# A fused two-block transformer kernel: one depthwise chunk moved to DVE, the others three chunks behind the projection, and unread products in TensorE's waits

## The chip, the cores and the metric

The kernel runs on one NeuronCore of one Trainium2 chip. The metric is the device time of one execution in microseconds; lower is better.

## The reference

256 tokens of width 1024, all in float32, pass through two blocks of two layers each. The part that the change touches is in the second block:

```python
def _conformer_conv(h, w_pw1, b_pw1, w_dw, b_dw, ln_g, ln_b, w_pw2, b_pw2):
    u = h @ w_pw1 + b_pw1                                   # 1024 -> 2048
    u = u[..., :D_MODEL] * jax.nn.sigmoid(u[..., D_MODEL:])
    c = depthwise_conv(u, w_dw, taps=31, centred) + b_dw    # each channel by itself
    c = jax.nn.silu(_layernorm(c, ln_g, ln_b))
    return c @ w_pw2 + b_pw2

def second_block(x):
    for i in range(2):
        x = x + 0.5 * rmsnorm(swiglu(rmsnorm(x)))           # half feed-forward
        m = conformer_conv(rmsnorm(x)) if i == 0 else diff_attention(rmsnorm(x))
        x = x + rmsnorm(m)
        x = x + 0.5 * rmsnorm(swiglu(rmsnorm(x)))
```

The first block has a layer with a compressed and windowed attention, one with a latent attention, and a feed-forward behind each. The differential attention is the third attention of the kernel.

## The kernel before

**Numbers.** Products have to be near float32. Every weight w is split into a high part that TensorE reads in one pass (`whi`) and the rest (`wlo`), every operand into `hthi` and `htlo`, and each product is made of three. ScalarE makes the high parts, DVE the low parts.

**Weights.** All weights come as a stream of 176 units of 128 x 3072 through `raw`, `whi` and `wlo`, two slots each, in two pieces: a (2048 columns) and b (1024). SyncE loads a piece when DVE has made the low part of the one before in its slot. Each engine's program is an order written out by hand; semaphores tie them together. `hi_a`, `hi_b` (ScalarE) and `lo_a`, `lo_b` (DVE) are the two splits of a unit.

**Borders.** Between two stages x has to be complete, is transposed by TensorE in four groups of four (`x_operand`, `operand_ahead`, L899), gained and split by ScalarE (L508) and DVE (L1436), and is then the operand. Groups 0 and 1 come first; group 2 stands in front of the first products, group 3 in front of the products of k = 2. At the borders numbered 5 to 9 (`AFTER_POST`: op_conv, op_f4, op_f5, op_qkv, op_f6) x is the sum of the old x and a normed output, which DVE adds in a first and a second half (L1510); groups 0 and 1 wait for the first, group 2 for the second. op_f4 and op_f6 follow a mixer, the others a feed-forward.

**Convolution stage.** The projection has 16 output groups q of 128 channels; q = 2c and 2c+1 are value and gate of chunk c (8 chunks). They lie in units as `PW1 = [[0,1,2],[3,4,5],[6,7,8],[9,10,11],[12,13],[14,15]]`. When q = 2c+1 is done, DVE scales the bank (L1876), ScalarE takes the sigmoid (L815), DVE multiplies (L1879) into `conv_u`. The depthwise convolution of a chunk is 32 small products on TensorE (`convolve`, L1272): GpSimd stores the chunk to DRAM (`gated`, L405) and loads it four times, shifted by a column each, into one of three slots (`stacked`, L412), so that a product covers four taps of 32 channels. The tap weights are eight loads of 512 KB, made long before. `convolve(c)` stands in TensorE's order two chunks behind the projection (`BEHIND = 2`). ScalarE adds the bias (`biased`, L803); the layer norm's mean and variance are products with a matrix of 1/1024 (L1281, L1321). Then DVE and ScalarE make the operand of the second pointwise product (`htlo`, L1897).

**Unread products.** `busy(cnt)` issues products whose results nobody reads; it stands once in the second attention's preparation (L891).

**Third attention.** 16 items; per item two score products on TensorE (L1098), bias and maximum on DVE (L1581), exponentials on ScalarE (L597), mixing on DVE (L1610), two transposes (L1107) and two value products (L1139). Scores run two items ahead. ScalarE is the busiest there.

```python
            for w, chunks in enumerate(PW1):
                ...
                    if q % 2 and q // 2 >= BEHIND:
                        convolve(q // 2 - BEHIND)
            taken("r_conv", 1)
            mean_of(range(0, 8 - BEHIND - 1))
            for c in range(8 - BEHIND, 8):
                convolve(c)
            mean_of(range(8 - BEHIND - 1, 8)).then_inc(ev["mean_done"], 1)
```

Of the kernel before, what the change touches and what calls it, by code (L numbers as in the profile page):

```python
# [60 lines left out]
BEHIND = 2  # L61
# [17 lines left out]
        ("qnope", 1), ("b_pw1", 16), ("ln_g", 8), ("ln_b", 8), ("b_dw", 8),  # L79
# [110 lines left out]
def build(nc, stream, cols_d, rows_d, wide_d, taps_d, x_d, const_d, out_d):  # L190
    ctx = ExitStack()
    with ctx:
# [38 lines left out]
        extra = sb("extra", [P, STACK * UPITCH])  # L231
# [7 lines left out]
        def col(name, i=0):  # L239
# [14 lines left out]
        tap_w = [(tr[:, 2048 + 1024 * c:3072 + 1024 * c] if c < 6 else att[:, 1024 * (c - 6):1024 * (c - 5)])  # L254
                 .rearrange("p (g q n) -> p g q n", g=STACK, q=SHIFTS) for c in range(8)]
# [4 lines left out]
        conv_bank = [acc[c % 4][:, (c // 4) * T:(c // 4 + 1) * T] for c in range(8)]  # L260
# [75 lines left out]
            "qpe_ready", "mean_done", "centred", "sq_ready", "var_done",  # L336
# [46 lines left out]
        def _(pool):  # L383
# [8 lines left out]
            for n in range(7):  # L392
                if n == 0:
                    pool.wait_ge(ev["cm1"], 1)
                if n == 2:
                    pool.wait_ge(s_ol, 16)
                    pool.wait_ge(s_x, 12)
                    for c in range(8):

                        pool.wait_ge(s_useb, U_F2 + 2 + 2 * c)  # L400
                        pool.dma_start(tap_w[c].rearrange("p g q n -> p (g q n)"), taps_d[c]).then_inc(s_tap, 16)
                if n == 3:
                    for c in range(8):
                        pool.wait_ge(s_glu, c + 1)
                        pool.dma_start(gated[c], conv_u[:, c, :]).then_inc(s_gtd, 16)  # L405
                        if c == 0:
                            pool.wait_ge(s_std, RSTD["n5"] + 1)
                        if c >= SLOTS:
                            pool.wait_ge(s_dw, c - SLOTS + 1)
                        pool.wait_ge(s_gtd, 16 * (c + 1))  # L410
                        for j in range(STACK):
                            pool.dma_start(stacked[c % SLOTS][j * GROUP:(j + 1) * GROUP, :, 0:UPITCH - STACK],  # L412
                                           gated[c].rearrange("(g p) n -> p g n", g=STACK)[:, :, j:j + UPITCH - STACK])\
                                .then_inc(s_stk[c % SLOTS], 16)
# [10 lines left out]
        def _(act):  # L425
# [374 lines left out]
            def biased(c):  # L800

                act.wait_ge(s_dw, c + 1)
                nc.scalar.activation(conv_c[:, c, :], conv_bank[c], ACT.Identity, bias=col("b_dw", c)).then_inc(s_cc, 1)  # L803

            for w, chunks in enumerate(PW1):
# [5 lines left out]
                for q in chunks:  # L811
                    if q % 2:
# [4 lines left out]
                        if c > BEHIND:  # L817
# [59 lines left out]
        def _(pe):  # L877
# [31 lines left out]
            def operand_ahead(name, src, there):  # L909
# [12 lines left out]

                one(0)
                one(1)
                return ready

            def x_operand(name, m):
# [6 lines left out]
                return operand_ahead(name, lambda t, c: x[:, t, c * P:(c + 1) * P], there)  # L934
# [138 lines left out]
            def attention(kind):  # L1073
# [70 lines left out]
                scores(1)  # L1144
                for i in range(cnt + 2):
# [118 lines left out]
            def convolve(c):  # L1264

                pe.wait_ge(s_tap, 16 * 8)
                pe.wait_ge(s_stk[c % SLOTS], 16 * STACK * (c // SLOTS + 1))
                if c >= 4:
                    pe.wait_ge(s_cc, c - 3)
                for q in range(SHIFTS):  # L1270
                    for g in range(STACK):
                        ins = nc.tensor.matmul(conv_bank[c][g * GROUP:(g + 1) * GROUP, :], tap_w[c][:, g, q, :],  # L1272
                                               stacked[c % SLOTS][:, g, STACK * q:STACK * q + T],
# [3 lines left out]
            def mean_of(chunks_):  # L1277

                for c in chunks_:
                    pe.wait_ge(s_cc, c + 1)  # L1280
                    ins = nc.tensor.matmul(mean_bank, ones, conv_c[:, c, :], start=c == 0, stop=c == 7)  # L1281
# [3 lines left out]
            for w, chunks in enumerate(PW1):  # L1285
# [3 lines left out]
                for m, q in enumerate(chunks):  # L1289
# [32 lines left out]
            ins.then_inc(ev["var_done"], 1)  # L1322

# [18 lines left out]
            attention("diff")  # L1342
# [8 lines left out]
        def _(dve):  # L1351
# [513 lines left out]
            V.memset(conv_u[:, :, PAD + T:], 0.0)  # L1865
# [220 lines left out]
```

## Time and profile before

| | |
|---|---|
| time, median of 3 runs | 1826.09 us (1823.67 to 1826.11) |
| the profiled execution | 1820.93 us, of it span 1819.1 us |
| TensorE busy | 1700.5 us, 93% of the span |
| DVE, ScalarE busy | 1135.2 us (62%), 821.7 us (45%) |
| GpSimd busy | 37.8 us (2%) |
| mean granted TensorE clock | 0.970 of full speed |

The span runs from the first to the last instruction of the profiled execution. A granted clock of 1.00 is TensorE at 2.4 GHz, 0.50 is 1.2 GHz; a value between is the mean over a stretch in which it changed. The convolution stage lies between 931 and 1067 us, the third attention between 1544 and 1578 us. In a row of a timeline, "x8" are eight instructions in one row, the second number is what they took together, and the bracket says how long the engine was idle before it and for whom.

### The profile page before, as it was taken

How to read it: one execution, taken by the hardware profiler on the slowest of the kernel's cores; microseconds unless marked ns; L12 is line 12 of the kernel's file. 1: busy time of each engine (PE TensorE's matmuls, PEld its weight loads, DVE VectorE, ACT ScalarE, POOL GpSimd, SP SyncE). 2: the span in 40 equal slices, each digit the busy share in tenths (PEclk: the TensorE clock that was granted, in tenths of full speed). 3: DMA queues.
4: the chain of work that ended last, by engine and by line, in shares of the span. 5: the costliest groups of instructions: out<-in, count | busy, mean ns of one | idle time of the engine just before them, and what ended most of it. 6: DMA issues, size and time to landing. Idle time of an engine off the chain costs nothing.

```text
span 1819.1 us, 29989 instructions
## 1 busy us (share of the span) xinstructions
PE 1700.5 (93%) x11719; PEld 1564.4 (86%) x11719; DVE 1135.2 (62%) x1646; ACT 821.7 (45%) x1236; POOL 37.8 (2%) x65
## 2 busy tenths in 40 slices
PE   7969999998999999999988789998999989789998
PEld 7947799997878999999987589997999989689997
DVE  4777566655756666766563366666656655666665
ACT  4466454335645433543352454334434354754333
POOL 0000000000000000000003110000000000000000
PEclk9979999999999999999999989999999999889999
DMA  7610255453425655454536345454445445045454
GB/s 272 207 60 1 70 178 201 175 182 128 141 71 199 227 208 204 154 208 173 187 140 195 106 162 208 173 191 166 174 175 201 177 137 185 3 139 208 173 194 152
DMA packets 56366, 295.88 MB, mean 163 GB/s; under 512 B 6640, under 2 KB 7024, under 8 KB 33776
## 3 DMA queue, kind: packets, MB, share of 16 engines
q1 hardware_dynamic: 52224, 281.33, 43.1%
q0 software_dynamic: 4080, 13.70, 2.5%
q8 instruction: 42, 0.69, 0.2%
q14 instruction: 20, 0.16, 0.0%
HBM read 292.77 MB, written 2.23 MB: 162 GB/s over the span
## 4 chain that ended last, share of the span: by engine, by line
PE 87%; DVE 6%; ACT 5%; issue 1%; DMA 1%; POOL 0%; DVEq 0%; SPq 0%; ACTq 0%; POOLq 0%
PE bank L880 18%; PE bank L882 18%; PE bank L881 18%; PE bank L1069 9%; PE bank L1038 3%; PE bank L1040 3%; PE bank L1042 3%; PE bank L899 2%; PE bank L1272 2%; PE bank L1127 1%; PE bank L1085 1%; PE bank L1107 1%; ACT att L597 1%; ACT whi L440 1%; DVE x L1510 1%
## 5 line engine op out<-in xcount | busy, mean ns | idle before, releaser
L880 PE MATMUL bank<-hthi,whi 128*128 128x256 f32 x2144 | 608.2, 284 | 0.0
L882 PE MATMUL bank<-hthi,wlo 128*128 128x256 f32 x2144 | 607.3, 283 | 0.0
L881 PE MATMUL bank<-htlo,whi 128*128 128x256 f32 x2144 | 607.3, 283 | 0.0
L1365 DVE TENSOR_TENSOR wlo<-raw,whi 128x2048 fp32r<-128x2048 f32 x175 | 401.1, 2292 | 103.1 <-ACT whi L440 103.1
L880 PEld LDWEIGHTS bank<-hthi,whi 128*128 128x128 f32 x2144 | 411.8, 192 | 6.7 <-issue 2.1
L881 PEld LDWEIGHTS bank<-htlo,whi 128*128 128x128 f32 x2144 | 411.8, 192 | 4.7
L882 PEld LDWEIGHTS bank<-hthi,wlo 128*128 128x128 f32 x2144 | 411.8, 192 | 0.0
L440 ACT ACTIVATE whi<-raw 128x2048 fp32r<-128x2048 f32 x175 | 334.0, 1908 | 38.7 <-PE bank L882 27.3
L523 ACT ACTIVATE tr<-tr 128x256 f32<-128x256 f32 x132 | 55.2, 418 | 641.8 <-DVE tr L1454 641.8
L1454 DVE TENSOR_TENSOR tr<-bank,rb 128x512 f32<-128x512 f32 x132 | 91.2, 691 | 225.6 <-PE bank L882 225.4
L1371 DVE TENSOR_TENSOR wlo<-raw,whi 128x1024 fp32r<-128x1024 f32 x174 | 212.2, 1219 | 28.4 <-ACT whi L448 28.2
L880 PE MATMUL bank<-whi,hthi 128*128 128x384 f32 (+4 forms) x520 | 175.1, 337 | 14.7 <-DVE htlo L1897 6.9
L448 ACT ACTIVATE whi<-raw 128x1024 fp32r<-128x1024 f32 x174 | 181.5, 1043 | 0.4 <-PE bank L882 0.3
L881 PE MATMUL bank<-wlo,hthi 128*128 128x384 f32 (+4 forms) x520 | 171.9, 331 | 0.0
L882 PE MATMUL bank<-whi,htlo 128*128 128x384 f32 (+4 forms) x520 | 171.8, 330 | 0.0
L880 PEld LDWEIGHTS bank<-whi,hthi 128*128 128x128 f32 (+1 forms) x520 | 99.5, 191 | 17.6 <-issue 10.1
L1038 PE MATMUL bank<-whi,hidhi 128*128 128x512 f32 x288 | 113.4, 394 | 0.0
L1040 PE MATMUL bank<-wlo,hidhi 128*128 128x512 f32 x288 | 112.9, 392 | 0.0
L1042 PE MATMUL bank<-whi,hidlo 128*128 128x512 f32 x288 | 112.1, 389 | 0.0
L881 PEld LDWEIGHTS bank<-wlo,hthi 128*128 128x128 f32 (+1 forms) x520 | 99.6, 191 | 0.0
L882 PEld LDWEIGHTS bank<-whi,htlo 128*128 128x128 f32 (+1 forms) x520 | 99.1, 191 | 0.0
L1457 DVE TENSOR_TENSOR tr<-tr 128x256 f32<-128x256 f32 x132 | 56.2, 426 | 63.9 <-ACT tr L523 63.9
(250 smaller groups left out, 1999.7 us busy)
## 6 DMA issues: line engine op xcount, KB each, us to landing
raw<-in_stream SPq DMA_DIRECT2D x176, 1024.0 KB, 5.5
raw<-in_stream SPq DMA_DIRECT2D x176, 512.0 KB, 3.6
wide<-in_wide POOLq DMA_DIRECT2D x7, 512.0 KB, 4.3
tr<-in_taps POOLq DMA_DIRECT2D x6, 512.0 KB, 3.6
xn<-gated POOLq DMA_DIRECT2D x12, 142.0 KB, 4.0
proj<-gated POOLq DMA_DIRECT2D x12, 142.0 KB, 3.1
gated<-proj POOLq DMA_DIRECT2D x8, 144.0 KB, 3.1
extra<-gated POOLq DMA_DIRECT2D x8, 142.0 KB, 3.4
```

Of the source, the lines that this page charges most:

```text
L440: nc.scalar.activation(whi[:, s, 0:UA], raw[:, s, 0:UA], ACT.Copy).then_inc(s_hia, 1)
L448: nc.scalar.activation(whi[:, s, UA:UNIT], raw[:, s, UA:UNIT], ACT.Copy).then_inc(s_hib, 1)
L880: nc.tensor.matmul(out, whi_, mhi, start=start, stop=False)
L881: nc.tensor.matmul(out, whi_, mlo, start=False, stop=False)
L882: return nc.tensor.matmul(out, wlo_, mhi, start=False, stop=stop)
L1038: nc.tensor.matmul(acc[2 * t + j][:, :], hidhi[:, b, lhs], whi[:, s, sl], start=start, stop=False, skip_group_check=True)
L1040: nc.tensor.matmul(acc[2 * t + j][:, :], hidhi[:, b, lhs], wlo[:, s, sl], start=False, stop=False, skip_group_check=True)
L1042: ins = nc.tensor.matmul(acc[2 * t + j][:, :], hidlo[:, b, lhs], whi[:, s, sl], start=False, stop=stop, skip_group_check=True)
L1069: ins = nc.tensor.matmul(acc[2 * t + j][:, :], a[:, 1, lhs], w[:, s, sl], start=False, stop=False, skip_group_check=True)
L1365: V.tensor_tensor(wlo[:, s, 0:UA], raw[:, s, 0:UA], whi[:, s, 0:UA].bitcast(F32), ALU.subtract)\
L1371: V.tensor_tensor(wlo[:, s, UA:UNIT], raw[:, s, UA:UNIT], whi[:, s, UA:UNIT].bitcast(F32), ALU.subtract)\
L1454: V.tensor_tensor(gu[:, j, :].rearrange("p (h n) -> p h n", h=2), gate_up_bank[j], both, ALU.mult)\
```

## The change

Five things are altered.

1. `BY_DVE = 1`: chunk 0 of the depthwise convolution is computed by DVE, 31 instructions on 128 x 256 (`conv_taps`), each adding one shifted and weighted copy to `conv_c`. They stand in DVE's order in runs of five (`AHEAD`) behind the gate product of chunks 1 to 6, and the last one behind chunk 7's. Chunk 0 is no longer stored, loaded and multiplied by TensorE.
2. `BEHIND = 3`: the other seven chunks' products stand three chunks behind the projection; the mean products are spread between them; the one of chunk 0 waits for the new event `conv_early`.
3. The third slot of `stacked` lies in `att` in place of `extra`, and the tap weights of chunk 7 in the other part of `att`.
4. `busy` takes the operand that it reads and the bank that it writes. Unread products are added: at the five borders of `AFTER_POST`, 18 in front of group 0 and 10 behind group 1; 40 behind the variance products; 24 in the third attention behind the scores of items 0 and 1; 24 behind the third attention.
5. The constants `cols` have 31 more columns, the tap weights of chunk 0.

```diff
-BEHIND = 2
+BY_DVE = 1
+AHEAD = 5
+BEHIND = 3
...
-        extra = sb("extra", [P, STACK * UPITCH])
...
-            xn[:, :, :].rearrange("p t n -> p (t n)")[:, 0:STACK * UPITCH], proj[:, 4352:4352 + STACK * UPITCH], extra[:, :])]
+            xn[:, :, :].rearrange("p t n -> p (t n)")[:, 0:STACK * UPITCH], proj[:, 4352:4352 + STACK * UPITCH], att[:, 1024:1024 + STACK * UPITCH])]
...
-                    for c in range(8):
+                    for c in range(BY_DVE, 8):
+                        n_ = c - BY_DVE
                         pool.wait_ge(s_glu, c + 1)
                         pool.dma_start(gated[c], conv_u[:, c, :]).then_inc(s_gtd, 16)
-                        if c == 0:
+                        if n_ == 0:
                             pool.wait_ge(s_std, RSTD["n5"] + 1)
-                        if c >= SLOTS:
-                            pool.wait_ge(s_dw, c - SLOTS + 1)
-                        pool.wait_ge(s_gtd, 16 * (c + 1))
+                        if n_ >= SLOTS:
+                            pool.wait_ge(s_dw, n_ - SLOTS + 1)
+                        pool.wait_ge(s_gtd, 16 * (n_ + 1))
...
-                        if c > BEHIND:
+                        if c - BEHIND - 1 >= BY_DVE:
                             biased(c - BEHIND - 1)
...
-            def busy(cnt):
+            def busy(cnt, of=hthi, out=gub[1]):
 
                 for _ in range(cnt):
-                    nc.tensor.matmul(gub[1][:, 0:T], hthi[:, 0, 0:P], hthi[:, 1, :], start=True, stop=True)
+                    nc.tensor.matmul(out[:, 0:T], of[:, 0, 0:P], of[:, 1, :], start=True, stop=True)
...
+                busy(spare[0], hidhi)
                 one(0)
                 one(1)
+                busy(spare[1], hidhi)
                 return ready
...
-                return operand_ahead(name, lambda t, c: x[:, t, c * P:(c + 1) * P], there)
+                return operand_ahead(name, lambda t, c: x[:, t, c * P:(c + 1) * P], there,
+                                     (18, 10) if m in AFTER_POST else (0, 0))
...
                 scores(0)
                 scores(1)
+                busy(spare, hidhi)
                 for i in range(cnt + 2):
...
-                    if q % 2 and q // 2 >= BEHIND:
+                    if q % 2 and q // 2 - BEHIND >= BY_DVE:
                         convolve(q // 2 - BEHIND)
             taken("r_conv", 1)
-            mean_of(range(0, 8 - BEHIND - 1))
-            for c in range(8 - BEHIND, 8):
-                convolve(c)
-            mean_of(range(8 - BEHIND - 1, 8)).then_inc(ev["mean_done"], 1)
+            convolve(5)
+            mean_of(range(BY_DVE, 4))
+            convolve(6)
+            pe.wait_ge(ev["conv_early"], 1)
+            mean_of(range(0, BY_DVE))
+            mean_of(range(4, 6))
+            convolve(7)
+            mean_of(range(6, 8)).then_inc(ev["mean_done"], 1)
             for c in range(8):
                 if c % 2 == 0:
                     pe.wait_ge(ev["sq_ready"], c // 2 + 1)
                 ins = nc.tensor.matmul(var_bank, ones, conv_s[:, c, :], start=c == 0, stop=c == 7)
             ins.then_inc(ev["var_done"], 1)
+            busy(40, hidhi)
...
-            attention("diff")
+            attention("diff", 24)
+            busy(24, hidhi, acc[3])
             step(U_WO, ready=operand_ahead("op_wo", lambda t, c: diff_o[:, t, c * P:(c + 1) * P],
...
+            def conv_taps(k0, k1, ready=None):
+
+                for k in range(k0, k1):
+                    for c in range(BY_DVE):
+                        w = col("w_dw", k * BY_DVE + c)
+                        if k == 0:
+                            ins = V.tensor_scalar(conv_c[:, c, :], conv_u[:, c, 0:T], w, col("b_dw", c), ALU.mult, ALU.add)
+                        else:
+                            ins = V.scalar_tensor_tensor(out=conv_c[:, c, :], in0=conv_u[:, c, k:k + T], scalar=w,
+                                                         in1=conv_c[:, c, :], op0=ALU.mult, op1=ALU.add)
+                    if ready is None or k < k1 - 1:
+                        own(ins)
+                if ready is not None:
+                    ins.then_inc(ready, 1)
...
+                        if c == BY_DVE:
+                            dve.wait_ge(s_glu, BY_DVE)
+                        if BY_DVE <= c < 7:
+                            conv_taps((c - BY_DVE) * AHEAD, (c - BY_DVE + 1) * AHEAD)
+            conv_taps((7 - BY_DVE) * AHEAD, TAPS, ready=ev["conv_early"])
             dve.wait_ge(ev["mean_done"], 1)
```

## Rows read from the trace of the kernel before

**Rows 1.** The page, part 1: busy time and share of the span, by engine

```profile
PE 1700.5 (93%) x11719; PEld 1564.4 (86%) x11719; DVE 1135.2 (62%) x1646; ACT 821.7 (45%) x1236; POOL 37.8 (2%) x65
```

**Rows 2.** Waits of TensorE: in total us, times, longest us

```profile
PE bank L899 <- DVE x L1510: 28.7, 10, 4.5
...
PE bank L899 <- DVE proj L1935: 4.2, 1, 4.2
...
PE bank L1272 <- issue: 1.8, 1, 1.8
```

**Rows 3.** Windows: us; busy PE, PEld, DVE, ACT, POOL; granted clock; DMA share, GB/s

```profile
935.00:937.40 2.40, 0.00 (x0) 0.01 (x1) 2.28 (x5) 0.82 (x3) 0.00 (x0) 0.64 0.31 111
...
1034.50:1041.30 6.80, 0.00 (x1) 0.00 (x0) 3.75 (x5) 4.13 (x7) 0.00 (x0) 0.76 0.00 0
...
1543.26:1546.67 3.41, 3.41 (x21) 2.96 (x19) 1.96 (x8) 3.29 (x7) 0.00 (x0) 1.00 0.92 310
```

**Rows 4.** Timeline of TensorE at the border before op_f5: start, us, instruction

```profile
1268.99 1.56 PE L899 MATMUL bank<-const,x 128*128 128x128 f32 x8 [3.13 <-DVE x L1510]
...
1272.91 1.08 PE L899 MATMUL bank<-const,x 128*128 128x128 f32 x4 [2.36 <-DVE x L1510]
...
1277.04 0.36 PE L1009 MATMUL bank<-hthi,whi 128*128 128x256 f32 x1
```

**Rows 5.** Timeline of TensorE: four small products at the high clock

```profile
949.26 0.60 PE L942 MATMUL bank<-const,rs 128*128 128x128 f32 x4
949.62 0.36 PE L880 MATMUL bank<-hthi,whi 128*128 128x256 f32 x1
```

**Rows 6.** The chain that ended last: unread products in the second attention's preparation

```profile
488.19 3.58 PE bank L891 x30
```

**Rows 7.** Timeline of TensorE at op_qkv and at the output projection

```profile
1470.08 1.09 PE L899 MATMUL bank<-const,x 128*128 128x128 f32 x4 [2.63 <-DVE x L1510]
...
1475.26 0.42 PE L880 MATMUL bank<-whi,hthi 128*128 128x384 f32 x1
...
1585.18 1.09 PE L899 MATMUL bank<-const,proj 128*128 128x128 f32 x4 [1.14 <-DVE htlo L1436]
...
1590.62 0.61 PE L880 MATMUL bank<-whi,hthi 128*128 128x384 f32 x1
```

**Rows 8.** Timeline of TensorE at the start of the third attention

```profile
1544.10 3.69 PE L1098 MATMUL bank<-tr 128*128 128x256 f32 x16
...
1548.37 0.44 PE L1107 MATMUL bank<-const,att 128*128 128x128 f32 x2 [0.57 <-DVE att L1610]
```

**Rows 9.** Timeline of TensorE: the first three depthwise chunks

```profile
963.78 4.93 PE L1272 MATMUL bank<-xn,tr 128*32 128x256 f32 x64 [5.29 <-DMA xn<-gated]
...
974.58 3.66 PE L1272 MATMUL bank<-proj,tr 128*32 128x256 f32 x64
...
984.12 3.66 PE L1272 MATMUL bank<-extra,tr 128*32 128x256 f32 x64
```

**Rows 10.** Timeline of DVE between the first projection chunks

```profile
954.45 2.29 DVE L1365 TENSOR_TENSOR wlo<-raw,whi 128x2048 fp32r<-128x2048 f32 x1 [0.58 <-ACT whi L440]
...
959.80 0.48 DVE L1879 SCALAR_TENSOR_TENSOR proj<-tr,cols 128x256 f32<-128x256 f32 x1 [0.58 <-ACT tr L815]
...
960.75 1.23 DVE L1371 TENSOR_TENSOR wlo<-raw,whi 128x1024 fp32r<-128x1024 f32 x1 [0.46 <-ACT whi L448]
```

**Rows 11.** Timeline of GpSimd: the depthwise stage's DMA issues

```profile
955.13 2.22 POOL L412 DMA_DIRECT2D xn<-gated  x4 [2.11 <-DMA gated<-proj]
...
964.20 2.19 POOL L412 DMA_DIRECT2D proj<-gated  x4 [4.94 <-DMA gated<-proj]
...
974.33 2.19 POOL L412 DMA_DIRECT2D extra<-gated  x4 [7.38 <-DMA gated<-proj]
...
995.81 0.56 POOL L405 DMA_DIRECT2D gated<-proj  x1 [3.82 <-DVE proj L1879]
...
998.42 2.19 POOL L412 DMA_DIRECT2D extra<-gated  x4 [2.04 <-DMA gated<-proj]
```

More of the change, by code:

```diff
@@ L78 @@
         ("b1", 4), ("pos", 32), ("w2", 256), ("kv_c_norm", 2), ("q_a_norm", 3), ("knope", 1),
[L79 removed]
+        ("qnope", 1), ("b_pw1", 16), ("ln_g", 8), ("ln_b", 8), ("b_dw", 8), ("w_dw", TAPS * BY_DVE),
         ("subln", 1)]
@@ L252, in build @@
         conv_r = proj[:, 6400:6912].rearrange("p (c n) -> p c n", c=2)
[L254 to L255 removed]
+        tap_w = {c: (tr[:, 2048 + 1024 * (c - BY_DVE):3072 + 1024 * (c - BY_DVE)] if c < 7 else att[:, 0:1024])
+                 .rearrange("p (g q n) -> p g q n", g=STACK, q=SHIFTS) for c in range(BY_DVE, 8)}
         stacked = [v.rearrange("p (g n) -> p g n", g=STACK) for v in (
[L258 removed]
+            xn[:, :, :].rearrange("p t n -> p (t n)")[:, 0:STACK * UPITCH], proj[:, 4352:4352 + STACK * UPITCH], att[:, 1024:1024 + STACK * UPITCH])]
         gated = nc.dram_tensor("gated", (8, P, UPITCH), F32, kind="Internal").ap()
[L260 removed]
+        conv_bank = {c: acc[(c - BY_DVE) % 4][:, (c - BY_DVE) // 4 * T:((c - BY_DVE) // 4 + 1) * T] for c in range(BY_DVE, 8)}
         mean_bank, var_bank = tp[0][:, 0:T], tp[1][:, 0:T]
@@ L335, in build @@
             "ckv_ready", "qa_ready", "k2_sq", "k2_ss", "q2_sq", "q2_ss", "k2n_ready", "q2n_ready", "kpe_ready",
-            "qpe_ready", "mean_done", "centred", "sq_ready", "var_done",
+            "qpe_ready", "conv_early", "mean_done", "centred", "sq_ready", "var_done",
             "conv_std", "lny_ready", "conv_hi", "conv_lo",
@@ L800, in biased @@
             def biased(c):
-                act.wait_ge(s_dw, c + 1)
+                act.wait_ge(s_dw, c - BY_DVE + 1)
                 nc.scalar.activation(conv_c[:, c, :], conv_bank[c], ACT.Identity, bias=col("b_dw", c)).then_inc(s_cc, 1)
@@ L907, in operand, with operand_ahead @@
                        lambda q: [(P, P, src(t, 2 * q + j)) for j in range(min(2, nchunks - 2 * q)) for t in range(NT)])
-            def operand_ahead(name, src, there):
+            def operand_ahead(name, src, there, spare=(0, 0)):
                 def one(q):
@@ L1071, in down_prev, with attention @@
                 ins.then_inc(s_useb, 1)
-            def attention(kind):
+            def attention(kind, spare=0):
                 base, cnt = ITEM0[kind], NITEM[kind]
@@ L1264, in convolve @@
             def convolve(c):
[L1266 to L1269, printed above, removed]
+                n_ = c - BY_DVE
+                pe.wait_ge(s_tap, 16 * (8 - BY_DVE))
+                pe.wait_ge(s_stk[n_ % SLOTS], 16 * STACK * (n_ // SLOTS + 1))
+                if n_ >= 4:
+                    pe.wait_ge(s_cc, n_ - 3)
                 for q in range(SHIFTS):
@@ L1279, in mean_of @@
                 for c in chunks_:
-                    pe.wait_ge(s_cc, c + 1)
-                    ins = nc.tensor.matmul(mean_bank, ones, conv_c[:, c, :], start=c == 0, stop=c == 7)
+                    if c >= BY_DVE:
+                        pe.wait_ge(s_cc, c - BY_DVE + 1)
+                    ins = nc.tensor.matmul(mean_bank, ones, conv_c[:, c, :], start=c == BY_DVE, stop=c == 7)
                 return ins
```

11 lines of the change are left out of this document (6 added, 5 removed).

## The prediction, made before the change was timed

> **What bounds the kernel now.** I read the page first: TensorE is busy for 93% of the span, DVE for 62% [rows 1], so the kernel goes as fast as TensorE's queue, and only its idle time and its slow time can be won. The view of waits, TensorE alone, then shows where it is idle: 28.7 us in ten waits for x at the block borders, 4.2 us after the third attention, 1.8 us before the last depthwise products [rows 2], and, by TensorE's timeline, 5.29 us before the first ones [rows 9]. The reader is to see that each is a chain on DVE, ScalarE or the DMA queues that TensorE can't shorten by itself. The third view is the granted clock by stretch: in the second wait of a border its mean is 0.64, so it falls from 2.4 to 1.2 GHz there, and in the layer norm's wait of 6.8 us, with TensorE at 0.00, it falls too, to a mean of 0.76 [rows 3]. So a wait costs twice: while it lasts, and in the products behind it.
>
> **Borders (five times, before op_conv, op_f4, op_f5, op_qkv, op_f6).** The change adds 18 unread products in front of the wait for the first half of x and 10 behind the first eight transposes. One such product takes 3.58/30 = 0.12 us at 2.4 GHz [rows 6], so they take 2.2 us and 1.2 us. The waits that hide them are 3.13 and 2.36 us at the border of op_f5 [rows 4]; the longest are 4.5 us [rows 2]. Nothing queued behind them comes later, as long as the clock is high when they begin, and it is, since the block before ends in back-to-back products. Cold they would take about twice as long, 10 then still under 2.36.
> What they may win: from the third group of transposes to the products behind the fourth the trace has 1277.04 - 1272.91 = 4.13 us [rows 4]: two groups of four transposes and twelve 128x256 products. At 2.4 GHz a group of four costs 949.62 - 949.26 = 0.36 us [rows 5], so the same work is 0.36 + 12 x 0.12 + 0.36 = 2.16 us, 2.0 us less. The third group itself can't start earlier, as it waits for DVE's second half of x. ScalarE and DVE make the operand a group at a time behind the transposes, so they move with them, and in the feed-forward loop behind them the view of waits has none for another engine. For op_qkv with 384 columns: 1475.26 - 1470.08 = 5.18 us [rows 7]; twelve products at 0.33 cold and, by the ratio 0.12/0.226 of the narrower ones, 0.177 warm give 0.36 + 2.12 + 0.36 = 2.84, 2.3 us less. Five borders: 4 x 2.0 + 2.3 = 10.3 us if the clock holds everywhere. At the two that follow a mixer the wait is longer (4.5 us is the longest [rows 2]); 18 products leave over 2 us of it empty, and I take 1.3 us off: 9.0 us. Bounds: 0, if the clock falls all the same, and 12.5, if it holds and the first eight transposes, cold there now, come 0.5 us sooner too at those two and some more.
>
> **Output projection.** 24 products (2.9 us) lie in the 4.2 us after the last attention item [rows 2], so they delay nothing when warm; cold they would reach about 1 us past it. Behind it 1590.62 - 1585.18 = 5.44 us [rows 7] would be 2.84: 2.6 us. But the stretch from the wait's end to the third group holds only transposes and another wait of 1.14 us [rows 7], with nothing put into it (operand_ahead is called without spare here). I take 2.0 us, bounds -1 and 3.5.
>
> **Start of the third attention.** 24 products come between the scores of item 1 and of item 2. Here TensorE is not waiting: it runs the scores of four items from 1544.10 for 3.69 us and idles only 0.57 us before the first transposes [rows 8]. 24 x 0.12 = 2.9 us less 0.57 makes the first item's transposes 2.3 us late; behind them ScalarE waits to copy them, and then the exponentials, which set the pace of the sixteen items. It catches up little. The granted clock is 1.00 there already [rows 3], so nothing comes back. I take 2.1 us lost, bounds 1.5 and 2.4.
>
> **Layer norm.** 40 products, 4.8 us, in a wait of 6.8 us [rows 3]. They delay nothing. What they can give is a high clock for the second pointwise product; its second half needs DVE's low part of the weights (1.23 us [rows 10]), which DVE makes only behind the operand, so most of the gain runs into that. Bounds 0 and 2, I take 0.5.
>
> **Depthwise stage.** Now chunk 0's products wait 5.29 us for their four loads and run cold, 4.93 us in place of 3.66; the period of a projection chunk with a depthwise chunk is 984.12 - 974.58 = 9.54 us, of which 48 projection products at 0.12 are 5.76, so a depthwise chunk costs 3.78 us [rows 9].
> Removed: chunk 0 from TensorE, 3.78; the wait, 5.29, since the first depthwise product is now that of chunk 1, and four groups (q6 to q9) stand before it; its cold clock, 1.27; the 1.8 us before the last chunk [rows 2], since between the last projection and chunk 7's products stand three depthwise chunks and six mean products, where the present order has two and five, 3.78 us and more of cover. Sum 12.1 us.
> Added on DVE: 31 taps on 128x256. The nearest row is the gate product of the same operation and shape, 0.48 us [rows 10]; from below 2.29/8 = 0.29 bounds it, an eighth of a subtraction on 2048 columns, from above 0.6, as each tap waits for the one before. I take 0.50, 2.5 us for a run of five. Two runs (chunks 1 and 2) come before DVE's low part of the last third of the unit, which now ends at 960.75 + 1.23 = 961.98 behind 0.47 us of waiting for ScalarE that the runs cover; it moves to 961.98 + 5.0 - 0.47 = 966.5. TensorE would reach q8 at 963.78 - 5.29 + 2 x 2.88 = 964.25 [rows 9]. So a new wait of about 2.3 us on DVE stands at q8. With depthwise products between, TensorE takes 3 x 2.88 + 1.5 x 3.78 = 14.3 us a unit. DVE's own work for two chunks, from 956.74 to 960.28, costs 1.77 us each [rows 10], so it takes 1.23 + 2.29 + 1.5 x (1.77 + 2.5) = 9.9, and no further wait follows. Chunk 0 on DVE is through some 10 us before TensorE asks for it (conv_early); behind that wait stand its mean product and chunk 7.
> The GpSimd queue: 5 issues a chunk (store, four loads), 35 in place of 40; the last wait of the queue, and the load of the next gain behind it, come no later. Chunk 0's loads took from their first issue at 955.13 to the product at 963.78, 8.65 us; chunk 1's are issued from 964.20, so it is there at 972.9, chunk 2's from 974.33, there at 983.0 [rows 9, 11]. TensorE asks at 966.5 + 2 x 2.88 = 972.3 and 9.54 later. Loss 1.1 us, bounds 0 and 3. Later, when the store lands faster, a chunk holds the queue only from 995.81 to 1000.61, 4.8 us [rows 11], half of TensorE's period. If the clock falls in the new wait at q8 that costs up to the 1.27 us of the row; I take 0.5.
> Stage: 12.1 - 2.3 - 1.1 - 0.5 = 8.2 us, bounds 4 and 12. The bank and slot waits (s_cc, s_dw) refer to products three or four chunks back and are met; extra's replacement in att is free then, one tap load less and 31 more columns of constants are hidden.
>
> **Sum.** 9.0 + 2.0 - 2.1 + 0.5 + 8.2 = 17.6 us. The profiled execution took 1820.93 us (span 1819.1 and 1.8 around it), so 1803.3 like for like; it lies 5.2 us under the median of the runs shown, 1826.09, from which I subtract: 1808.5 us.
>
> **A rule against the change.** While DVE's subtraction with two SBUF inputs ran (2.29 us), GpSimd's four issues from 955.13 took 2.22 us, and the four from 974.33, with DVE idle, 2.19 [rows 11]: no contention to be seen. The Trainium skill (GPSIMD Engine Reference, Key points) says that GpSimd shares its SBUF interfaces with VectorE and contends with DVE instructions that have two SBUF inputs, as each tap has. By that rule the issues would be held by the taps; by the row not at all. The sum goes by the row.
>
> **Rivals.**
> 1. The clock falls all the same: eight transposes stand between the two waits [rows 4] and didn't hold it, and the products leave holes in each wait. Then the borders, the output projection and the layer norm give nothing: 8.2 - 2.1 = 6.1 us, 1820.0. For it: the holes of the long waits. Against it: at a plain border 0.9 and 1.2 us stay empty. Chance 0.17.
> 2. The projection without depthwise products between is fed too slowly: DVE with the taps, or loads that land later behind the denser weight stream. The stage gives 4 us in place of 8.2: 1812.7. Chance 0.11.
> 3. The other side: DVE's taps hold GpSimd's issues, five a chunk. At 1 us each (two taps) a chunk holds the queue 4.8 + 5 = 9.8 us and its loads land 2 to 4 us behind that, some 12 us a chunk with the slow stores: chunk 7 is there at 983.0 + 5 x 12 = 1043, where TensorE asks for it at 983.0 + 2 x 9.54 + 3 x 3.78 and some means, 1016. 27 us lost against 17.6 won: 1835.5. It decides from 10.2 us a chunk, about 0.65 us an issue. Against it: the row above, two equal fours of issues. Chance 0.04. The Trainium skill's rule (GPSIMD Engine Reference, Key points) is what speaks for this rival.
> 4. The change doesn't do what it says: gains and the attention's loss cancel within the noise, 1826. Chance 0.05.
> My forecast, gain 12 to 24 us: 0.61; the rest, 0.02, is more gain.
>
> **Numbers.** 1808.5, its own range 1802 to 1814. For 8 in 10 it reaches to most of rival 1 and, on the low side, to the profiled execution's lower level: 1799 to 1821. 0.2% is 3.7 us, about what a measurement of this kernel can tell from no change; beyond it faster 0.91 (forecast, rivals 1 and 2, more), within it 0.05, slower 0.04.
>
> **What would show it.** TensorE's waits for x no longer than now and twelve products behind the third transposes in 1.4 us; a granted clock of 1.00 there; no wait for xn<-gated and one of about 2.3 us for DVE's wlo L1371 near 962; the first depthwise product near 971; the mean done about 9 us earlier, the border's 2 us aside; the first transposes of the third attention 2.3 us later behind its scores. Wrong if the clock column shows 0.50 at the borders, if a tap takes 0.6 us or more, or if chunk 1's loads land 5 us late.

## The result, and the profile after

The changed kernel takes 1801.11 us (median of 4 runs, 1799.44 to 1805.47), the one before in the same session 1824.88 (4 runs, 1820.52 to 1826.11): ratio 0.9866, 95% interval 0.9848 to 0.9883. That is 23.8 us less; forecast were 17.6 less, and 1808.5 us with a range of 1799 to 1821. So the measured median lies inside that range, but 0.9 us below the narrower one of 1802 to 1814 that the forecast called its own. The profiled executions differ by less than the medians: 1820.93 against 1802.5 us, 18.4.

The page of the changed kernel, busy time by engine, and the granted clock in 40 slices:

```profile
PE 1712.7 (95%) x11883; PEld 1579.6 (88%) x11883; DVE 1149.4 (64%) x1677; ACT 820.4 (46%) x1235; POOL 34.4 (2%) x59
...
PEclk9979999999999999999999999999999999999999
```

TensorE has 164 instructions more than in [rows 1] and is busy 12 us longer in a shorter span: busy time now holds unread work, so it no longer says how near the kernel is to its bound. The view of waits says it, TensorE alone:

```profile
PE bank L902 <- DVE x L1525: 10.9, 9, 2.3
...
PE bank L883 <- DVE htlo L1933: 2.1, 1, 2.1
...
PE bank L1280 <- issue: 0.3, 1, 0.3
```

The 28.7 us of waiting for x [rows 2] are now 10.9 (filled by 28 unread products a border, not gone), and the waits for xn<-gated [rows 9] and for proj before op_wo [rows 2] have left the list. In their place, TensorE's timeline in the depthwise stage:

```profile
965.28 0.39 PE L883 MATMUL bank<-hthi,whi 128*128 128x256 f32 x1 [2.15 <-DVE wlo L1386]
...
971.22 3.66 PE L1280 MATMUL bank<-xn,tr 128*32 128x256 f32 x64
...
1013.88 3.66 PE L1280 MATMUL bank<-xn,att 128*32 128x256 f32 x64 [0.34 <-issue]
...
1020.26 3.72 PE L1334 MATMUL bank<-proj,const 128*128 128x256 f32 x16 [1.44 <-ACT proj L827]
```

Against [rows 9]: no wait before the first depthwise products, which run in 3.66 us and not in 4.93, and a new wait of 2.15 us on DVE at the third group of the unit. Windows of the changed kernel (columns as in rows 3), at op_conv's second wait, behind the layer norm's unread products, at op_f4, op_f5, the third attention's start and its end:

```profile
935.50:937.90 2.40, 1.15 (x10) 0.94 (x8) 2.26 (x5) 0.84 (x3) 0.00 (x0) 1.00 0.31 113
...
1031.00:1035.80 4.80, 4.80 (x19) 4.79 (x20) 3.04 (x5) 4.71 (x9) 0.00 (x0) 0.64 0.02 3
1062.80:1069.80 7.00, 6.28 (x32) 6.01 (x32) 3.44 (x8) 1.70 (x5) 0.00 (x0) 0.53 0.23 75
1259.80:1262.50 2.70, 1.45 (x13) 1.24 (x11) 2.26 (x5) 1.14 (x4) 0.00 (x0) 1.00 0.30 109
1529.60:1534.30 4.70, 4.70 (x34) 4.49 (x34) 2.43 (x11) 4.17 (x12) 0.00 (x0) 1.00 0.48 197
1561.00:1567.60 6.60, 6.21 (x28) 5.92 (x29) 0.89 (x4) 5.30 (x18) 0.00 (x0) 0.50 0.00 0
```

The clock is 1.00 where it was 0.64 [rows 3], but in this execution it still falls to 1.2 GHz in three places: behind the layer norm, at op_f4, and in the last items of the attention. Products that run at 1.2 GHz are called cold below, those at 2.4 GHz warm.

**Where the 18.4 us are.** From the starts of the same instructions in both traces, stretch by stretch (before, after, gain): op_conv's first transposes to the variance products 97.28, 86.25, **11.03**; from there to op_f4's first transposes 40.53, 40.50, 0.03; to op_f5's 197.68, 197.85, **-0.17**; to op_qkv's 197.01, 195.16, 1.85; to op_wo's 116.08, 115.42, 0.66; to op_f6's 34.24, 31.18, 3.06; to the end 202.78, 200.33, 2.45. Ahead of op_conv the changed kernel was 0.51 later in this execution. Sum 18.4. "The stage" is the first of these stretches from here on. It is read from one trace of each kernel, and executions differ in it too: the changed kernel, e3 and e8 have the same code up to the variance products and take 86.25, 88.08 and 87.01 us; e5 and e10 have the same, and take 87.18 and 88.35. A difference of under 2 us between two traces is therefore not shown by them alone.

### The profile page after: what moved, and what is told of

Read it like the earlier page. It is cut to its first block, busy times and chain, and to the rows that moved or that the text cites. A ratio compares the mean times of both kernels' runs of the same rounds, so it can differ in the third digit from the quotient of the medians.

```text
span 1800.7 us, 30346 instructions
## 1 busy us (share of the span) xinstructions
PE 1712.7 (95%) x11883; PEld 1579.6 (88%) x11883; DVE 1149.4 (64%) x1677; ACT 820.4 (46%) x1235; POOL 34.4 (2%) x59
## 4 chain that ended last, share of the span: by engine, by line
PE 87%; DVE 6%; ACT 5%; issue 1%; DMA 0%; DVEq 0%; SPq 0%; ACTq 0%
PE bank L883 18%; PE bank L885 18%; PE bank L884 18%; PE bank L1075 9%; PE bank L1044 4%; PE bank L1046 3%; PE bank L1048 3%; PE bank L902 2%; PE bank L1133 1%; PE bank L1280 1%; PE bank L1091 1%; ACT whi L443 1%; PE bank L1113 1%; PE bank L894 1%; ACT att L600 1%
```

## Experiments

**Halves: e1 and e2.** Edit of e1 (changed kernel):

```diff
-                                     (18, 10) if m in AFTER_POST else (0, 0))
+                                     (0, 0))
...
-            busy(40, hidhi)
...
-            attention("diff", 24)
-            busy(24, hidhi, acc[3])
+            attention("diff")
```

> The changed kernel without all unread products that the change added (borders, layer norm, start of the third attention, before op_wo); the depthwise part stays. Theory A (my terms: borders 9.0, output projection 2.0, layer norm 0.5, attention -2.1): 9.4 us slower than the changed kernel, about 1810.5; from the third transposes of a border to the products behind the fourth 4.1 us again with the granted clock near 0.6, the scores-to-last-transposes stretch of the third attention 31.7 us in place of 33.3. Theory B (the depthwise stage gave nearly all, the unread products only fill idle time): within 3 us of the changed kernel, 1801 to 1804.

e2 is the kernel before with all these unread products put in, and nothing else.

> The kernel before with all the unread products of the change and its own depthwise stage (two chunks behind, none on DVE). Theory A: the two halves are independent, so this gains what the other one loses, 9 us: about 1815.5, and every border gives what it gives in the changed kernel. Theory B (unread products matter little): 1822 to 1825.

e1: 1814.95 us against 1825.71 for the kernel before on the same chip, ratio 0.9939 (0.9918 to 0.996): 10.8 us for the depthwise part alone. e2: 1812.3, ratio 0.9932 (0.9908 to 0.9957): 13.4 us for the unread products alone. The two add up to 24.2, the whole change gave 23.8. Theory B is dead for both. Theory A has the places right and the sizes too small: it expected 1810.5 and 1815.5, and both halves gave more at the medians than forecast, 10.8 against 8.2 and 13.4 against 9.4. The stage takes 89.12 us in e1, 8.16 less than in the first trace of the kernel before.

**Distance against DVE's chunk: e5 and e6.** e5 is e2 with BEHIND = 3; e6 is the changed kernel with BEHIND = 2 (chunk 5 then falls into the loop, and the means are regrouped).

> The kernel of e2 (the one before with all unread products) with the depthwise products three chunks behind in place of two, chunk 0 still on TensorE. Theory A (distance and DVE's chunk are two separate terms): of the 6.9 us wait for the loads before the first depthwise products 1.1 stays, the cold clock of those products (1.3) and the wait of 1.2 before the last chunk go, the 3.8 us of chunk 0 stay: 7 to 8 us faster than e2, about 1805. Rival (the distance only moves the wait to the next chunk's loads, since GpSimd's queue gives a chunk no faster): a wait for gated of several us stays before chunk 0 or comes before chunk 1, and the gain is under 3 us.

> The changed kernel with chunk 0 on DVE, but the depthwise products two chunks behind. Theory A: chunk 1's products are asked for 5.8 us earlier, its loads come no earlier, so a wait for xn<-gated of 5 us comes before them, the clock falls in it (1.3 us) and a wait of about 1 us comes before the last chunk: 4 to 7 us slower than the changed kernel, about 1807. Rival (DVE's chunk is what matters): within 2 us of it.

e5: 1801.89 us (0.9868, 0.9842 to 0.9893), the same as the changed kernel, with all eight chunks on TensorE. Its stage takes 87.18 us, e2's 96.59: the distance gives 9.4 us by this pair of traces and 10.4 at the medians, a little more than expected. The chunk on DVE then gives only 0.93 (to 86.25), which is within what executions differ by: that it gives anything in this order is not shown, that it doesn't give its 3.7 us is. e6: 1811.6 us (0.9915, 0.9887 to 0.9944), stage 95.82, 9.6 over the changed kernel's and more than the 4 to 7 expected. TensorE's timeline of e6:

```profile
970.07 6.08 PE L1280 MATMUL bank<-xn,tr 128*32 128x256 f32 x64 [5.81 <-DMA xn<-gated]
...
1018.24 5.35 PE L1280 MATMUL bank<-att,tr 128*32 128x256 f32 x64 [2.00 <-issue]
```

Both waits are there, and behind each the same 64 products run in 6.08 and 5.35 us in place of 3.66. Without the distance DVE's chunk is worth 0.8 us (96.59 to 95.82), again no more than the scatter.

**What holds DVE's chunk back: e4, e7, e9, e10.** e4 moves the taps behind the wait of q8:

```diff
-AHEAD = 5
+AHEAD = 7
...
-                        if BY_DVE <= c < 7:
-                            conv_taps((c - BY_DVE) * AHEAD, (c - BY_DVE + 1) * AHEAD)
-            conv_taps((7 - BY_DVE) * AHEAD, TAPS, ready=ev["conv_early"])
+                        if 3 <= c < 7:
+                            conv_taps((c - 3) * AHEAD, (c - 2) * AHEAD)
+            conv_taps(4 * AHEAD, TAPS, ready=ev["conv_early"])
```

> The changed kernel with DVE's taps moved: none behind chunks 1 and 2, seven each behind chunks 3 to 6, the last three behind chunk 7. Theory A (two runs of taps in front of DVE's low part of the weights make TensorE's wait of 2.15 us at q8): that wait is gone, chunk 1's loads are there, the mean is done 2.1 us earlier, about 1799.0. Rival: chunk 1's four loads, issued behind the stores, then end the wait instead, 1 to 2 us of it stay as a wait for xn<-gated, and the whole is within 1 us; or the longer runs of taps (3.6 us) hold a later chunk's gate and a new wait comes at q14 to q15.

It came out slower than the changed kernel: 1807.58 us (0.9904, 0.9881 to 0.9927), stage 91.71. TensorE:

```profile
970.59 3.66 PE L1280 MATMUL bank<-xn,tr 128*32 128x256 f32 x64 [2.49 <-DMA xn<-gated]
982.34 5.35 PE L1280 MATMUL bank<-proj,tr 128*32 128x256 f32 x64 [2.14 <-DMA proj<-gated]
...
1013.02 3.66 PE L1280 MATMUL bank<-att,tr 128*32 128x256 f32 x64 [0.89 <-issue]
```

The wait on DVE is gone, and the rival's wait for the loads stands in its place with all of its size; my 2.1 us were never there to win. What I had not expected at all is the second one. GpSimd's timeline of the changed kernel, and then of e4:

```profile
957.59 0.55 POOL L408 DMA_DIRECT2D gated<-proj  x1 [23.79 <-DVE proj L1910]
963.34 2.21 POOL L415 DMA_DIRECT2D xn<-gated  x4 [5.21 <-DMA gated<-proj]
965.54 0.57 POOL L408 DMA_DIRECT2D gated<-proj  x1
971.33 2.18 POOL L415 DMA_DIRECT2D proj<-gated  x4 [5.22 <-DMA gated<-proj]
...
979.96 2.18 POOL L415 DMA_DIRECT2D att<-gated  x4 [5.89 <-DMA gated<-proj]
...
1009.21 2.18 POOL L415 DMA_DIRECT2D xn<-gated  x4 [6.65 <-DMA gated<-proj]
```

```profile
971.04 2.19 POOL L415 DMA_DIRECT2D proj<-gated  x4 [5.58 <-DMA gated<-proj]
973.22 0.56 POOL L408 DMA_DIRECT2D gated<-proj  x1
982.87 2.18 POOL L415 DMA_DIRECT2D att<-gated  x4 [9.09 <-DMA gated<-proj]
...
999.27 2.18 POOL L415 DMA_DIRECT2D proj<-gated  x4 [8.27 <-DMA gated<-proj]
```

The bracket is GpSimd waiting for its own store to land. In both kernels every store but the first goes out right behind the loads of the chunk ahead: the queue is a serial chain of store, landing and four loads, and never waits for DVE again. In the changed kernel it keeps up narrowly (the last loads are issued at 1009.21 for products at 1013.88); in e4 it doesn't. But the queue is only part of it. The wait of 2.14 us stands before chunk 2's products, and its loads were issued at 971.04, no later than in the changed kernel (971.33), where the products began at 980.76 without a wait; in e4 the loads took 11.3 us from their first issue to the products at 982.34. That wait and the cold products behind it are 3.8 of the 5.5 us that e4's stage is longer. The stores of 9.1 and 8.3 us are those of chunks 3 and 5, and only the small waits before chunks 5 to 7 lie behind them. In e4 SyncE issues two weight loads at 969.57 and 971.78, in the changed kernel at 972.99 and 975.20; that they held up chunk 2's loads is likely and not shown.

e7 breaks that chain in e4, with two semaphores by turns:

```diff
-                        pool.wait_ge(s_glu, c + 1)
-                        pool.dma_start(gated[c], conv_u[:, c, :]).then_inc(s_gtd, 16)
+                        if c < 8:
+                            pool.wait_ge(s_glu, c + 1)
+                            pool.dma_start(gated[c], conv_u[:, c, :]).then_inc(s_gtd[c % 2], 16)
...
-                        pool.wait_ge(s_gtd, 16 * (n_ + 1))
+                        pool.wait_ge(s_gtd[(c - 1) % 2], 16 * (n_ // 2 + 1))
```

> The kernel of e4 (taps late) with GpSimd issuing the store of the next chunk before it waits for the landing of this one's (two semaphores by turns, nothing else). In e4 GpSimd waited 9.1 us for one store to land and 8.3 for another while the four loads stood behind. Theory A (the serial chain store, landing, loads on GpSimd's queue is what sets the pace of the stage): the waits of e4 at chunks 2, 5, 6 and 7 and the cold chunk 2 go, 5 us faster than e4, about 1802.5; the wait of 2.5 us at the first chunk stays, as nothing stands ahead of it. Rival (the DMA engines themselves are full with the weight stream): the stores land that much later, and it stays within 1.5 us of e4.

1801.98 us (0.9866, 0.9842 to 0.9891), 5.6 under e4's median; stage 86.54, 5.2 us under e4's: theory A in size. It shows that an earlier issue covers the landings (chunk 2's loads go out at 968.23), not that the queue had made them long. That is the level of the changed kernel (86.25 to 88.08), so late taps and early stores together gave nothing over it yet; early stores with the taps of the changed kernel were not run. Only the first chunk's wait is left (3.05 us). e9 then puts chunks 1 and 2 both behind q11, and takes the attention's products out and 36 ahead of op_f4:

```diff
-                    if q % 2 and q // 2 - BEHIND >= BY_DVE:
-                        convolve(q // 2 - BEHIND)
+                    if q == 11:
+                        convolve(1)
+                    if q >= 11 and q % 2:
+                        convolve(q // 2 - BEHIND)
```

> The changed kernel with everything that the runs so far point to: taps late and stores ahead as in e7, and both chunk 1 and chunk 2 put behind the twelfth projection group (q11), so that chunk 1's loads have 5.8 us more; no unread products at the start of the third attention, 36 ahead of op_f4. Theory A (with the loads there, each microsecond taken off TensorE's queue counts): no wait in the stage but the one for the variance, from the first transposes of op_conv to the variance 83.3 us in place of 86.3 in the changed kernel, 1.6 from the attention and 2 at op_f4: about 1796. Rival (the denser queue of TensorE meets the weight stream, whose loads or low parts come late): waits for DVE's wlo appear at q12 to q15, and the stage stays at 86 us.

> The kernel of e5 (chunk 0 on TensorE, three behind, no work of the stage on DVE) with the same unread products as e9: none at the third attention, 36 ahead of op_f4. Theory A: the stage takes 87.2 us as in e5, 3.8 more than in e9, since there the loads are fed: about 1800 less the 1.6 of the attention, 1798 to 1799. Rival: DVE's chunk gives nothing in any order, and e9 and e10 have the same stage.

e9: 1797.54 us (5 runs, 1796.44 to 1798.24; ratio 0.9842, 0.9828 to 0.9857), faster than both kernels: all of its runs lie under all of the changed kernel's. Part of that is its unread products; e8 below has the same ones but for 16 more in the layer norm, and e9 is 3.2 us under it. Its stage takes 83.17 us, and TensorE's timeline has no wait above 0.2 us in it but the variance's:

```profile
975.86 3.66 PE L1283 MATMUL bank<-xn,tr 128*32 128x256 f32 x64
...
1012.07 3.66 PE L1283 MATMUL bank<-xn,att 128*32 128x256 f32 x64
1018.46 3.72 PE L1339 MATMUL bank<-proj,const 128*128 128x256 f32 x16 [1.44 <-ACT proj L830]
```

e10: 1799.43 us (0.9859, 0.9841 to 0.9877), stage 88.35 with 1.48 us of waiting before the last chunk. So between the stages of e10 and e9 lie 5.2 us, where DVE's chunk gives the changed kernel 0.9. By their duration 3.7 of them are the 64 products, and the rest is that wait, which the stores ahead of e9 might have removed without DVE's chunk too. This is argued and not shown: e9 and e10 also differ in the order of the products and of the stores, and e10 with those two was not run. The medians are only 1.9 us apart: in the two traces e9 came 1.9 us later to op_conv and lost 2.0 us between op_qkv and op_f6, where the products behind its third transposes for op_wo ran cold.

**The unread products place by place: e3, e8, e11.** e3 takes out the 24 at the third attention; e8 also gives op_f4 36 and the layer norm 56.

> The changed kernel without the 24 unread products at the start of the third attention alone. Theory A (they stand in front of the scores of item 2 and the first transposes, and ScalarE's pace carries the delay to the last item): the stretch from the first scores to the last transposes is 31.7 us in place of 33.3, the whole 1.6 us faster, about 1799.5. Rival: they hold the clock or come out of idle time later, and the stretch stays at 33.3 or the clock falls before it; no faster or slower.

> The changed kernel with other counts of unread products: none at the start of the third attention, 36 in place of 18 ahead of op_f4 (where 2.33 us stayed empty and the clock fell), 56 in place of 40 in the layer norm (where 2.1 us stayed empty). Theory A: 1.6 us from the attention, 2.0 at op_f4 (products behind the third and fourth transposes at full clock), up to 1 in the layer norm: about 1797. Rival: the clock falls at other times in any case (the runs show falls at different places), and only the 1.6 us are there: 1799.5.

> One look for the trace. The changed kernel with only the 18 products ahead of the first transposes at op_f4 and op_qkv, only the 10 behind them at op_conv, op_f5 and op_f6, and 48 in place of 24 at the start of the third attention. Theory A: 10 alone hold the clock at the three borders where the first wait is 3.1 us or less (the clock is still high at its end), 18 alone don't at the other two, since the second wait of 2.4 us is empty again; the scores-to-last-transposes stretch of the third attention grows by another 2.9 us, to 36.2. Rival: both are needed, and all five borders are cold from the third transposes on, 4.1 us for the twelve products.

The third attention, TensorE's timeline of the changed kernel, then of e11 (48 products):

```profile
1529.62 1.97 PE L1104 MATMUL bank<-tr 128*128 128x256 f32 x8
1531.23 3.22 PE L894 MATMUL bank<-hidhi 128*128 128x256 f32 x24
1534.29 1.89 PE L1104 MATMUL bank<-tr 128*128 128x256 f32 x8
...
1562.93 0.69 PE L1113 MATMUL bank<-const,att 128*128 128x128 f32 x2 [0.31 <-DVE att L1625]
```

```profile
1530.70 1.97 PE L1104 MATMUL bank<-tr 128*128 128x256 f32 x8
1532.31 6.10 PE L894 MATMUL bank<-hidhi 128*128 128x256 f32 x48
...
1566.91 0.44 PE L1113 MATMUL bank<-const,att 128*128 128x128 f32 x2 [0.97 <-DVE att L1625]
```

First scores to last transposes: 31.71 us before (1575.81 against [rows 8]) and without the products in e9, 33.31 with 24, 36.21 with 48. The second 24 cost their full 2.9 us, the first 24 1.6. Nothing comes back. e3 as a whole: 1799.23 us (0.9863, 0.9836 to 0.989), on the side of theory A, though medians can't tell 1.6 us apart; the timeline can.

The borders. At op_f4, the changed kernel and then e8:

```profile
1060.76 1.45 PE L902 MATMUL bank<-const,x 128*128 128x128 f32 x8 [2.33 <-DVE x L1525]
1061.96 2.00 PE L894 MATMUL bank<-hidhi 128*128 128x256 f32 x10
1064.68 1.08 PE L902 MATMUL bank<-const,x 128*128 128x128 f32 x4 [0.72 <-issue]
...
1074.90 0.60 PE L948 MATMUL bank<-const,rs 128*128 128x128 f32 x4
```

```profile
1063.15 1.45 PE L902 MATMUL bank<-const,x 128*128 128x128 f32 x8 [0.17 <-DVE x L1525]
...
1067.08 0.63 PE L902 MATMUL bank<-const,x 128*128 128x128 f32 x4 [1.28 <-DVE x L1525]
...
1075.16 0.61 PE L948 MATMUL bank<-const,rs 128*128 128x128 f32 x4
```

From the first transposes to the rows' product (L948) 14.14 us in the changed kernel, as much as before (13.97), and 12.01 in e8: 18 products leave 2.33 us of the wait empty, the clock falls while the next 10 run (2.00 us in place of 1.43), 36 leave 0.17 and it holds, in e8 as in e9 and e10. With 18 it is a matter of the execution. In e2, e3, e4, e5 and e7 the 10 products ran cold too (2.12 to 2.48 us), but the clock was back for the products behind the fourth transposes; in e6 it never fell. All six gain 1.5 to 2.0 us there (e2, e5 and e7 take 196.20, 195.86 and 196.00 us to op_f5's first transposes); of the seven traces with 18 and 10 only the changed kernel's has nothing. e8 as a whole took 1800.7 us (0.9857, 0.9833 to 0.9881), not the 1797 of theory A, though its trace has both gains: the clock fell at the variance products (5.41 us in place of 3.72), and the layer norm gave nothing. The 56 products fill the wait to 0.23 us, but a wait of 0.93 us for DVE's low part of the weights follows, as one of 0.96 does in e3, where the clock held with 40.

e11 (one run, 1806.06 us) has only the 10 at op_conv, op_f5 and op_f6, and only the 18 at op_f4 and op_qkv. At op_f5 and at op_qkv:

```profile
1259.06 2.35 PE L894 MATMUL bank<-hidhi 128*128 128x256 f32 x10
1261.78 1.03 PE L902 MATMUL bank<-const,x 128*128 128x128 f32 x4 [0.37 <-issue]
1264.08 0.60 PE L902 MATMUL bank<-const,x 128*128 128x128 f32 x4
...
1457.50 1.09 PE L902 MATMUL bank<-const,x 128*128 128x128 f32 x4 [2.63 <-DVE x L1525]
1461.50 0.60 PE L902 MATMUL bank<-const,x 128*128 128x128 f32 x4
```

At op_f5 the 10 alone run cold themselves (2.35 us) but leave 2.3 us between the third and fourth transposes, close to the 1.9 of both together; at op_f5 that is 1.5 of 1.9 us won. The 18 alone leave 4.00 at op_qkv, where both give 2.55 and the kernel before has 4.73: 0.7 of 2.2 us won. The 18 alone gave nothing at op_f4 (3.44 us between third and fourth transposes), and the 10 alone all of the 1.6 us at op_conv and 2.2 of 2.5 at op_f6. The 10 are the part that pays; theory A was right on that, and half right on the clock, which the 10 hold at op_conv and at op_f5 and op_f6 don't hold but bring back.

**Why the medians say more than the profile: e12.**

> The kernel before, unchanged, for a second trace: the profiled execution of the first one took 1820.9 us, 4 to 5 under the medians. Theory A (executions differ in work ahead of the change, and the first one was a fast one): op_conv's first transposes come 1 to 3 us later than at 933.5, the stretch from there to op_f6's (682.8 us) stays within 1 us. Rival: the stretch itself differs between executions, with a longer wait for the first depthwise loads (e2 had 6.9 in place of 5.3).

1828.51 us (one run). op_conv's first transposes at 934.36, 0.9 later than in the first trace; the stretch to op_f6's 689.5 us, not 682.8. Theory A has fallen, the rival holds. TensorE:

```profile
964.94 6.45 PE L1272 MATMUL bank<-xn,tr 128*32 128x256 f32 x64 [5.58 <-DMA xn<-gated]
1027.91 5.35 PE L1272 MATMUL bank<-proj,att 128*32 128x256 f32 x64 [2.88 <-issue]
```

The stage took 101.83 us, 4.55 more than in the first trace: the same 64 products in 6.45 us in place of 4.93 [rows 9], a last wait of 2.88 in place of 1.8 [rows 2] and cold products behind it. The seven traces with the products three behind and no edit of taps or stores (changed kernel, e1, e3, e5, e8, e10, e11) lie between 86.25 and 89.12. So the change also took away a wait whose size differs between executions, and the prediction rested on a mild one: against this second trace e1's stage is 12.7 us shorter and the changed kernel's 15.6, not 8.2 and 11.0. The other 2.1 us of the longer stretch lie behind the stage. Whether that is all of the 5.4 us between 23.8 and 18.4 stays open: there are two traces of the kernel before.

## Why the prediction was right, step by step

- **Borders**, forecast 9.0. Measured from the first transposes to the rows' product or the fourth transposes: op_conv 1.6, op_f4 -0.2, op_f5 1.9, op_qkv 2.2, op_f6 2.5, sum 8.0. Right in mechanism and size but for op_f4; "the clock is high when they begin" was right, and the empty part of the long wait, for which I took 1.3 us off at two borders, costs op_f4 all of its gain in the changed kernel's trace and at most 0.5 us in six others. At op_f6 the wait was never 4.5 us long: that was op_f4's, op_f6's was 3.60, 1.45 of it stayed empty and the clock held. The waits for x were filled, and nothing behind them came later.
- **Output projection**, forecast 2.0: 3.06. I left out that the first eight transposes now run warm, in 1.09 us in place of 1.97. The first 2.6 us of the 24 products themselves ran at 0.50 of the clock, as it had fallen in the attention's last items.
- **Start of the third attention**, forecast -2.1: -1.6, and e11 shows the mechanism by its slope.
- **Layer norm**, forecast 0.5: 0.03 in the trace, 0.36 where the clock held (e3). There it runs into a wait of 0.96 us for DVE's wlo, as written.
- **Depthwise stage**, forecast 8.2: 8.16 by e1, where nothing else is in it; 11.03 in the changed kernel with the border's 1.6 and a clock that held in the wait at q8. The first product was forecast near 971 and came at 971.22, the wait on wlo at 2.3 and came at 2.15. Of the two smaller losses the 1.1 us for the loads were never lost (they were there in time in both), and the clock, booked at 0.5, fell in e1 behind the wait at q8 and took about 1.5. That 8.16 meets 8.2 to a few hundredths is therefore in part chance, all the more as it is measured against the milder trace of the kernel before. The border alone gives the old stage only 0.7 (e2): there TensorE merely comes sooner to a wait that grows from 5.3 to 6.9 us.
- **Inside the stage one reason was too simple.** "TensorE asks at 972.3" against loads there at 972.9 makes two limits that lie within a microsecond, DVE's wlo and the loads. I booked them as two losses and called later chunks safe, since a chunk then "holds the queue only 4.8 us". That was the queue of before, which waits for DVE's gate. Here stores wait for nothing but each other's landing, a chunk takes 5.7 to 9.4 us of the queue, and its lead over TensorE shrinks from 5.7 us at chunk 1 to 2.5 at chunk 7. e4 lost 6.5 us with that little lead, as loads landed late, and e7, which alters the queue alone, has 5.6 of them back.
- **Rivals.** 1 (the clock falls all the same) happened at one border of five in this execution. 2 (slow feeding) didn't in the changed kernel, and did in e4: chunk 2's loads landed late, which is the second of its reasons, and the serial queue, which I didn't give, left no room for it. 3 (taps hold GpSimd's issues) is dead. The four issues from 963.34, beside the end of the taps and then a subtraction with two SBUF inputs, took 2.21 us; the four from 1009.21, with DVE idle, 2.18: 0.55 us an issue either way. The Trainium skill (GPSIMD Engine Reference, Key points) says that such DVE instructions contend with GpSimd; for its DMA issues no run here shows it.
- **A tap**, taken at 0.50 us, took 0.51, from DVE's timeline:

```profile
961.40 2.56 DVE L1890 SCALAR_TENSOR_TENSOR proj<-proj,cols 128x256 f32<-128x256 f32 x5
```

- **Size.** Trace against trace the forecast was 0.8 us off (17.6 against 18.4). So near a hit is luck: the terms were off by more, and part of them cancelled: op_f4 and the layer norm gave 2 less, the output projection and the attention 1.6 more. At the medians 23.8 us were won, 6.2 more than forecast, since the sum stood on one mild execution of the kernel before; it stayed in the range because the range was wide. e12 points to that kernel's waits for the other 5.4 us, but doesn't show all of them.

## What to carry to other kernels

Before you take work off the busiest engine, look for the second limit right behind the first: here the chunk on DVE was worth at most 0.9 us, no more than executions differ by, until loads and order were mended; what it is worth afterwards (3.7 us by the duration of its 64 products) was not run by itself. A queue that stores, waits for the landing and loads again is a serial chain; issue the next store before waiting for this one, and most of the chain's latency is off TensorE's path (5.2 us in e7 against e4); the first chunk still waits for its own. Unread products pay in the last wait before dense work, not in front of work that is already on time, and a wait that they fill only in part gives its gain in some executions only.

## What the runs showed of the hardware

- The wait of GpSimd for a store of 144 KB to land ran from 2.04 to 7.38 us within one execution [rows 11] and up to 9.09 us in e4, beside the weight stream. The changed kernel's trace has 2.91 to 6.65 us; e11, whose stage differs only by the 18 products ahead of it, has up to 8.25 us. What makes a landing long is not shown.
- The clock behind a partly filled wait differs between executions of the same unread products. At op_f4 it was back for the fourth transposes' products in e2, e3, e4, e5 and e7, had never fallen in e6, and stayed low in the changed kernel. Behind the layer norm e3 and e10 held it (1.00), where the changed kernel and e9 show a mean of 0.64 over 4.8 us, by that mean about 3.5 us at 1.2 GHz.
- Products that run cold can still bring the clock back: the 24 ahead of op_wo ran from 1564.98 in 4.33 us (3.12 in e3), the window over the first 2.6 us of them shows 0.50, and the eight transposes behind them took 1.09 us, the time of full clock.
